# mLSTM sample states on paired row tiles over five banks, sample numerators on paired column tiles, earlier next scores, and one FFN panel half moved ahead of a copy

## The reference, cut to what matters

```
num   = S @ v + decay * (q @ C)                    # per sequence b, C of (128, 256)
C_new = carry_decay * C + einsum(w_s, k, v)        # over the 8 tokens of b
```

## Time and profile before

| What | Value |
|---|---|
| Median of 3 runs | 2567.34 us (2565.26 to 2567.75) |
| Profiled execution, its own time | 2565.75 us |
| Span of its trace | 2563.8 us |
| Mean granted TensorE clock | 0.989 |
| Busy: PE, PE weight loads | 2473.5 us (96%), 2355.3 us (92%) |
| Busy: DVE, ACT, POOL | 1684.0 us (66%), 1073.0 us (42%), 307.7 us (12%) |
| Chain that ended last, by engine | PE 87%, DVE 7%, ACT 3%, issue 2%, POOL 1% |

### The profile page before, as it was taken

One profiled execution on the slowest core, in us unless ns is written; L12 is line 12 of the kernel. 1 busy time (PEld: TensorE's weight loads), 2 busy tenths in 40 slices (PEclk: granted clock), 3 DMA queues, 4 the chain that ended last, 5 costly groups with the idle time before them and its releaser, 6 DMA issues.

```text
span 2563.8 us, 45161 instructions
## 1 busy us (share of the span) xinstructions
PE 2473.5 (96%) x17653; PEld 2355.3 (92%) x17653; DVE 1684.0 (66%) x2398; ACT 1073.0 (42%) x1780; POOL 307.7 (12%) x247
## 2 busy tenths in 40 slices
PE   6999999999899999999998999999999999999998
PEld 5999999877688999999998999999997789999998
DVE  6676675888555586848568585765434586857666
ACT  6444353455333453525445353443133354443532
POOL 0000001202330100000030000001322200000012
PEclk9999999999899999999999999999999999999999
DMA  4233232222232222333222333332323222332322
GB/s 121 83 99 91 83 94 78 52 49 75 72 110 77 58 79 87 99 87 94 84 78 78 91 91 91 90 91 71 92 69 103 87 66 82 99 99 82 96 76 72
DMA packets 410806, 216.44 MB, mean 84 GB/s; under 512 B 40085, under 2 KB 407834, under 8 KB 410650
## 3 DMA queue, kind: packets, MB, share of 16 engines
q1 hardware_dynamic: 404646, 209.17, 29.0%
q10 hardware_dynamic: 2420, 3.37, 0.4%
q0 software_dynamic: 3584, 1.84, 0.4%
HBM read 206.57 MB, written 7.76 MB: 84 GB/s over the span
## 4 chain that ended last, share of the span: by engine, by line
PE 87%; DVE 7%; ACT 3%; issue 2%; POOL 1%; DMA 0%; SPq 0%; ACTq 0%; DVEq 0%; POOLq 0%
PE ps L2461 13%; PE ps L2463 13%; PE ps L2466 13%; PE ps L2523 12%; PE ps L2524 12%; PE ps L2525 12%; PE ps L1010 2%; DVE st L628 1%; PE ps L924 1%; POOL wlo L1739 1%; PE ps L886 1%; PE ps L875 1%; PE ps L1563 1%; PE ps L972 1%; PE ps L994 1%
## 5 line engine op out<-in xcount | busy, mean ns | idle before, releaser
L1739 POOL TENSOR_TENSOR wlo<-raw,whi 128x1024 fp32r<-128x1024 f32 (+2 forms) x96 | 207.6, 2163 | 1823.0 <-ACT whi L1794 1823.0
L1794 ACT ACTIVATE whi<-raw 128x1024 fp32r<-128x1024 f32 (+2 forms) x175 | 169.4, 968 | 433.1 <-PE ps L2466 432.1
L2461 PE MATMUL ps<-uh,whi 128*128 128x320 f32 (+1 forms) x1408 | 302.2, 296 | 8.0 <-POOL wlo L1739 7.3
L2463 PE MATMUL ps<-ul,whi 128*128 128x320 f32 (+1 forms) x1408 | 301.1, 295 | 0.0
L2466 PE MATMUL ps<-uh,wlo 128*128 128x320 f32 (+1 forms) x1408 | 301.1, 295 | 0.0
L2461 PEld LDWEIGHTS ps<-uh,whi 128*128 128x128 f32 x1408 | 215.9, 188 | 10.7 <-issue 10.5
L2228 DVE TENSOR_TENSOR ub<-ps,r 128x576 f32<-128x576 f32 x96 | 72.7, 757 | 230.7 <-PE ps L2466 215.0
L2466 PEld LDWEIGHTS ps<-uh,wlo 128*128 128x128 f32 x1408 | 216.0, 188 | 0.0
L2463 PEld LDWEIGHTS ps<-ul,whi 128*128 128x128 f32 x1408 | 216.0, 188 | 0.0
L2147 DVE TENSOR_TENSOR wlo<-raw,whi 128x1024 fp32r<-128x1024 f32 x88 | 107.8, 1225 | 130.3 <-ACT whi L1814 130.3
L2461 PE MATMUL ps<-xh,whi 128*128 128x320 f32 x752 | 164.2, 300 | 3.3 <-DVE RB L1280 2.7
(11 more groups left out here) (425 smaller groups left out, 7085.3 us busy)
## 6 DMA issues: line engine op xcount, KB each, us to landing
raw<-in_w_ffa_in SPq DMA_DIRECT2D x88, 512.0 KB
raw<-in_w_ffb_in SPq DMA_DIRECT2D x88, 512.0 KB
raw<-in_w_ffa_out SPq DMA_DIRECT2D x32, 512.0 KB
pages<-in_cache_ckv SPq DMA_DIRECT2D x128, 128.0 KB, 2.0
raw<-in_w_ffb_out SPq DMA_DIRECT2D x32, 512.0 KB
raw<-in_w_mlstm_in SPq DMA_DIRECT2D x24, 512.0 KB
raw<-in_w_ple_gate SPq DMA_DIRECT2D x16, 512.0 KB
raw<-in_w_ffa_out SPq DMA_DIRECT2D x16, 384.0 KB
```

The costliest lines, as they stand in the source:

```text
L1739: pool.tensor_tensor(lo[:, 0:n, :], raw[:, p % RAW, 0:n, :], hi[:, 0:n, :].bitcast(F32), ALU.subtract).then_inc(wlo_ready, 1)
L1794: act.activation(hi[:, 0:n, :], raw[:, p % RAW, 0:n, :], ACT.Copy).then_inc(whi_ready, 1)
L2461: mm(out[:, t], hi[:, n, :], xh_n[:, t], start=first and n == 0, stop=False)
L2463: mm(out[:, t], hi[:, n, :], xl_n[:, t], start=False, stop=False)
```

## The change

Five edits in the mLSTM and one in the FFN:
1. `sample_numerators`: every product writes 32 token rows in place of 64. The first one is split in two; sequences k and k+4 follow each other, on token rows 0 to 31 and 32 to 63.
2. `states`: every product sums over the 32 tokens that hold its sequence in place of 64, and sequences go in the order 0, 4, 1, 5, 2, 6, 3, 7; the carries follow that order.
3. Banks: B2, B3, B4 and the two of the gate panels' slot, then B2 and the slot's two again. `states(h, 0)` waits for the gate panel's evacuation; the sixth, seventh and eighth states wait for one, four and five carries. Odd gate panels and the output projection wait for all eight carries.
4. `scores(h+1)` waits for six carries of head h.
5. FFN, ACT: for the last block of a part, `upper` of the first output panel moves ahead of the fourth copy, with its wait.

```
+        def batch_of(k):
+            return k // 2 + NB // 2 * (k % 2)
+
+        def state_out(k):
+            free = 2 * (LT % 2)
+            return ps[:, (B2, B3, B4, free, free + 1, B2, free, free + 1)[k], 0:DV + 1]
...
                 dve.wait_ge(l_cs, NB * h + b + 1)
-                dve.scalar_tensor_tensor(out=Cb[:, b, :], in0=Cb[:, b, :], scalar=dec[:, h % 2, TS + b:TS + b + 1],
-                                         in1=ps[:, (B2, B3, B4)[b % 3], 0:DV + 1], op0=ALU.mult, op1=ALU.add).then_inc(l_cn, 1)
+                at = batch_of(b)
+                dve.scalar_tensor_tensor(out=Cb[:, at, :], in0=Cb[:, at, :], scalar=dec[:, h % 2, TS + at:TS + at + 1],
+                                         in1=state_out(b), op0=ALU.mult, op1=ALU.add).then_inc(l_cn, 1)
...
                 if c:
                     pe.wait_ge(tile_taken, IT + 16 + c)
+                    if c > 2 and c % 2:
+                        pe.wait_ge(l_cn, NB * (c // 2))
...
                 if h:
-                    pe.wait_ge(l_cn, NB * h)
+                    pe.wait_ge(l_cn, NB * h - 2)
...
-                out = ps[0:TS, B5, 0:DV + 1]
-                mm(out, SD[h % 2][0:TS, 1280:1280 + TS], Vt[0:TS, 4, h, :], start=True, stop=False)
-                for b in range(NB):
-                    ins = mm(out, qdm[:, b * TS:(b + 1) * TS], Cb[:, b, :], start=False, stop=b == NB - 1)
+                half = TS // 2
+                for o in (0, half):
+                    mm(ps[o:o + half, B5, 0:DV + 1], SD[h % 2][0:TS, 1280 + o:1280 + o + half], Vt[0:TS, 4, h, :],
+                       start=True, stop=False)
+                for k in range(NB // 2):
+                    for b, o in ((k, 0), (k + NB // 2, half)):
+                        ins = mm(ps[o:o + half, B5, 0:DV + 1], qdm[:, b * TS + o:b * TS + o + half], Cb[:, b, :],
+                                 start=False, stop=k == NB // 2 - 1)
...
             def states(h, b):
 
-                if b >= 3:
-                    pe.wait_ge(l_cn, NB * h + b - 2)
-                mm(ps[:, (B2, B3, B4)[b % 3], 0:DV + 1], kwb[0:TS, b, :], Vt[0:TS, 4, h, :], start=True, stop=True).then_inc(l_cs, 1)
+                if b == 0:
+                    pe.wait_ge(tile_taken, IT + min(19 + 2 * h, 24))
+                if b >= 5:
+                    pe.wait_ge(l_cn, NB * h + (1, 4, 5)[b - 5])
+                at = batch_of(b)
+                rows = slice(0, TS // 2) if at < NB // 2 else slice(TS // 2, TS)
+                mm(state_out(b), kwb[rows, at, :], Vt[rows, 4, h, :], start=True, stop=True).then_inc(l_cs, 1)
...
                 pe.wait_ge(tile_taken, LT + (k - 1 if k else 0))
+                if not k:
+                    pe.wait_ge(l_cn, NB * LH)
...
+                        if not more:
+                            act.wait_ge(w_done, 7 * (g - 1) + 4)
+                            upper(part.p, 0, part.n)
                         copied(part, i, 4, 5, D_, B)
...
-                        if not more:
-                            act.wait_ge(w_done, 7 * (g - 1) + 4)
-                            upper(part.p, 0, part.n)
```

## The result

The changed kernel takes 2535.47 us (median of 4 runs, 2533.27 to 2538.84), against 2566.30 for the kernel before on the same chip (4 runs, 2564.12 to 2567.75): ratio 0.9882 [0.9865, 0.9899], 30.8 us less where 22.9 were forecast. Its profiled execution took 2538.84 us, with a span of 2536.9 and a mean granted clock of 0.986.

What follows compares the result with a forecast made beforehand. The prediction took TensorE's own queue, 87% of the span, as the bound. 14.2 us from the mLSTM heads plus 8.7 from the FFN made 22.9 off the median 2567.34: 2544.4 us, range 2540.5 to 2554.5.

Steps and rivals of the forecast that it cites:

- Part 1: mLSTM sample numerators: pairs on two column tiles run side by side, 16 turns become 8, 1.76 us less per head.
- No pairing: Rival, mLSTM: tiles run one after the other, so only banks, earlier scores and the FFN help; 2556.6 us, chance 8%.
- go by the row: mLSTM order of instructions: trust the earlier trace's 1.14 us for four tiles, sum 14.2 us; the in-order rule gives 11.6.
- Part 2: mLSTM states and next scores: paired row tiles and more banks; with the numerators, scores 3.7 us earlier, head 3 gains 3.1.
- 0.6 us of cover is left, so the whole 3.7 us stays: mLSTM transposes: scalings end at 1928.75, before transposes could start at 1929.35, so the scores' gain stays whole.
- Part 3: End of FFN parts: earlier upper half removes PE's 1.09 us loss in eight 8-block parts, 8.7 us; 6-block parts give 0.
- Half the change: Rival: the FFN edit gives nothing since the second panel or the upper half's landing sets the start; 2553.1 us, 12%.
- 8.7 us (bounds 0 ... and 10): Sum for the FFN parts' ends; bound 0 if the second panel were the limit everywhere, upper bound 10.
- 48 passes x 0.133: FFN output panels: PE's first tile takes 6.4 us, so the second panel keeps 0.3 us of cover.
- the term of 14.2 for the heads: mLSTM: numerators, states and scores together, 3 x 3.7 + 3.1 us over the four heads.
- The lower end of the range: Whole kernel: 2540.5 us, from small bounds in favour, 1.2 + 1.2, and the runs' spread, 2.5 us.
- The slower rival: mLSTM heads: narrow tiles leave most of the array idle and TensorE's clock falls to 1.2 GHz; 2584 us, chance 3%.

Runs made afterwards that it cites:

- experiment 3: The changed kernel with the sample numerators 64 token rows wide again, one after the other: 2545.22 us, ratio 0.9914 to the kernel before.
- experiment 4: The changed kernel with each state product over all 64 tokens again; order, banks and waits kept: 2542.57 us, ratio 0.9898 to the kernel before.
- experiment 7: The changed kernel with POOL's lower half of gate panel 2h+4 moved behind the pieces of the gated output: 2534.12 us, ratio 0.9872.
- experiment 1: The kernel before with the FFN edit alone: 2550.20 us, ratio 0.9938 to the kernel before.
- experiment 2: The changed kernel with the FFN edit undone, so the mLSTM edits alone: 2555.82 us, ratio 0.9946 to the kernel before.
- experiment 6: The changed kernel with the next scores waiting for the eighth carry again: 2537.24 us, ratio 0.9876 to the kernel before.
- experiment 9: The changed kernel with states on three banks only and scores behind the eighth carry; column and row tiles stay: 2546.97 us, ratio 0.9919.
- experiment 10: The changed kernel once more, unaltered: 2536.53 us, ratio 0.9882 to the kernel before.
- experiment 8: The kernel of experiment 7 with the denominators' product and scalings ahead of carries 6 and 7: 2534.16 us, ratio 0.9865 to the kernel before.
- experiment 11: The same kernel as experiment 8, run again: 2533.87 us, ratio 0.9871 to the kernel before.

## Why the prediction was right and wrong

- **Part 1, the numerators: right.** 1.76 us per head forecast; 3.69 - 1.93 = 1.76 in the groups, 1.8 to 1.9 by taking it out (experiment 3). Pairs on two column tiles run side by side in this order of two-pass products. "No pairing" is dead.
- **The instruction order: right to go by the row.** The Trainium skill, PSUM — Partial Sum Buffer, "Engine vs sequencer instructions", has products start and complete in program order; by that the 8 instructions of the first four states would need five turns. They took 1.14 us, like the earlier trace rows, and 2.00 as soon as they stood on the same rows (experiment 4). The trace does not agree with that working. It does not show whether the two passes of a product stand in PE's order as one instruction or two, so the page's sentence itself is not refuted here.
- **Part 2, up to the scores: right.** 7.3 us forecast, 7.32 measured.
- **Part 2, "0.6 us of cover is left, so the whole 3.7 us stays": wrong by 0.3 to 0.4 us per head.** The 1.5 us from the last carry to the scalings' end was read at a time when POOL stood still. With the carries 3 us earlier the product at L1457 came to lie under POOL's lower half and took 1.13 us in place of 0.16. Cost: 3 x 3.7 became 10.1. Experiment 7 shows the cause. The Trainium skill, SBUF — State Buffer, "Who interferes with whom", says that VectorE's second pair of ports is shared with GpSimd under an exclusive lock; the trace agrees: L1457, which reads two operands in SBUF, ends 0.02 us behind POOL's instruction whether that makes it 1.13 or 0.25 us long, while the carries, which take one from PSUM, kept their 0.44 us beside the same POOL instruction (1.75 us for four). The list of what the scores and the scalings are queued behind was complete; the list of what runs beside them at the new time was not made.
- **Part 3, starts: right.** 1.08 us per part for 1.09, and 0.08 on the pass behind it; the second panel kept its place in parts of 8 and took all back in parts of 6. "Half the change" is dead: the FFN edit alone gives 17.1 us.
- **Part 3, the sum "8.7 us (bounds 0 ... and 10)": this is the step that failed**, and with it the time and the range. It took the streams' own pace as the same on both sides ("48 passes x 0.133"). The stop of about 1.1 us ahead of a stream also decided, in half of the cases, on 133.3 or 130.0 ns for each of its passes. Removing the stop removed the draw: 8.4 us beside the 9.2. The term of 8.7 measures 17.1 us by itself (experiment 1) and 17.6 in the ledger; the term of 14.2 for the heads measures 12.9 in the profiles (11.5 by the medians of experiment 2), so an error of 1.3 the other way hides a part of the miss. The evidence lay in the trace of before: the same passes counted 227 in one window and 233 in another. A prediction that compared the streams with each other would have found 4 of 8 slow and asked what differs at their start.
- **The lower end of the range does not follow from its own terms.** 2544.4 less 1.2, 1.2 and 2.5 is 2539.5 and not 2540.5; the measured 2535.47 lies below both.
- **The slower rival: not borne out.** Heads 0 to 2 had a clock of 1.00 in every profile but two (head 2 of experiment 6, head 1 of experiment 9). Head 3 is where the clock falls, but not with pairs alone: over the 30 us from its first L1575 (now L1589) on it was 0.94 before and 0.89 in experiment 1, with the old heads, and 0.72 to 0.94 in the kernels with pairs (0.77 in the first profile after, 0.94 in experiment 10, the same kernel). At 0.94 this costs about 30 x 0.06 = 2 us at most, at 0.72 some 8. In the changed kernel's profile it fell at 1991.3, behind 2.2 us in which PE had nothing to do ahead of head 3; the kernel before has the same 2.2 us there (2.16 us ahead of L1573 at 2015.42) and kept 1.00 until 2028.3. A fall so close behind the start of head 3 stands only in profiles with pairs (the first after, experiments 2, 4, 8, 9 and 11), but the old heads have two profiles in all. Whether the narrow tiles do it was not tried and stays open.

## What to carry to other kernels

Price a stop of PE ahead of a long stream twice: its own length, and the pace that the stream behind it may take; compare equal streams of one trace by their count in equal windows, for a mean over them hides two kinds. When a step moves earlier, list not only what it waits for but what runs beside it at the new time, above all GpSimd beside VectorE instructions with two operands in SBUF. And take one profile of a change for one draw of the clock: here two of the same kernel differed by 3.3 us in one head alone.

## What the hardware showed beside

- Passes of alternately 320 and 256 columns have two stable paces, 130.0 and 133.3 ns, at a granted clock of 1.00 and with PE never idle. Joined to the passes before them without a stop, streams of 384 passes took 130.0 in 80 of 80; with a stop of 0.2 to 1.2 us they took 133.3 in 12 of 24. What inside TensorE holds the pace was not found.
- Products on paired tiles (32 columns or 32 rows each) overlap fully even as two-pass fp32: 16 in 1.93 us (3.69 unpaired), 8 in 1.14 (2.00 unpaired).
- A VectorE product of 128x5 elements took 1.13 us beside GpSimd's 128x1024 subtraction and ended with it, and 0.16 without it.
